# Short convolution, input projection: two 512-token products per weight slot, or seven products of halves

## The chip, the cores and the metric

The kernel runs on one core of one Trainium2 chip. The metric is the device time of one execution in microseconds (us), as the median of the runs shown. A difference of under about 0.2% (5.7 us here) can't be told from no change.

The engines are named as in the profile. PE is TensorE (PEld its weight loads), DVE is VectorE, ACT is ScalarE, POOL is GpSimd and SP is SyncE. SPq, DVEq and the like are the sequencers of these engines.

## What is computed

The program is a stack of six layers on 512 tokens of width 1024, all in float32. The first block has four attention layers. The second has a hybrid attention and state-space layer with a feed-forward layer, then a short convolution with a feed-forward layer. The change concerns the short convolution alone:

```python
def shortconv_mixer(h, w_in, conv_w, w_out):
    gb, gc, u = jnp.split(h @ w_in, 3, axis=-1)
    return (gb * dw_conv(gc * u, conv_w)) @ w_out
```

Here `h` is 512 x 1024 and `w_in` is 1024 x 3072, `dw_conv` is a depthwise convolution over tokens with three taps, and `w_out` is 1024 x 1024. The feed-forward layers, `(silu(h @ w_gate) * (h @ w_up)) @ w_down` with 2816 hidden columns, matter because they already use the scheme that the change brings to `h @ w_in`.

## The kernel before

Activations are held transposed, with 128 features on the partitions and tokens along the row. `h` has eight such tiles, and `T` is 512 tokens. PSUM has eight banks of 512 columns. Weights arrive through `ring`, two slots of 1 MB each. `load` on SP waits for the semaphore `slot_begun` and then issues the transfer into the slot that was freed. PE raises `slot_begun` at the first matmul that reads a slot.

**The short convolution, before.** Its weights are twelve slots of 256 output columns. They come in four groups `g`, each in the order gc, u, gb (`for part in (1, 2, 0)`, L623). On PE, `short_convolution` (L1680) runs `pair_of_tiles` (L739) for each slot: two tiles of 128 outputs in the two PSUM banks `TB`, and eight products over the 1024 inputs for each tile (L727). A float32 matmul leaves two records in the trace, so a slot is 32 records of 512 columns. ACT copies the gc tiles to `sc_gate` (L2247, recorded at L1769). DVE (L3150) multiplies each u tile by its gate into `sc_pad` (L3161), runs `convolve` (L2854, recorded at L2856 to L2858: a tensor_scalar and two scalar_tensor_tensor over 512 columns), and multiplies each gb tile by the result into `og` (L3169). The output projection (`out_projection_of_parts`, recorded at L921) reads `og`.

**The scheme of seven products.** In `ffn` (PE: L1627), a chunk is one slot: 1024 inputs by 256 outputs, for 512 tokens. Weights and activations are each cut into four quarters. DVE forms four sums of weight quarters for each slot (`sum_weights`, L3015, recorded at L3024, L3026, L3029 and L3031), and once for each layer four sums of activation quarters (`sum_moving`, L3037, recorded at L3044). PE then makes seven products of 512 inputs by 128 outputs by 256 tokens where a plain product would need eight (`first_parts` L1603, `other_parts` L1608, recorded at L1588). A part is 8 records of 256 columns, and a chunk is 56. Three results must be saved between parts. ACT copies them to `snaps` (L2225), and DVE adds them back (L3070, L3075 and L3077 in `gated_pair`). The last part of a chunk (`c.a22`, `t4`) waits until DVE has made the second of these additions (L1624). Two sets of three PSUM banks alternate.

In DVE's order of work, the four weight sums for the *next* chunk stand between the first and the second addition of the present one, and they wait until the next slot has arrived:

```python
nc.vector.tensor_tensor(put[0][:, early], r3, snaps[i][0], ALU.add).then_inc(S["sum_read"], ...)  # L3070
if i or not first:
    sum_weights(1 - i, 4)                                                                          # L3072
dve.wait_ge(S["part_done"], at.now(p7))
dve.wait_ge(S["snap_read"], snapped.now(4 * i + 3))
nc.vector.tensor_tensor(put[1][:, late], r1, snaps[i][2], ALU.add).then_inc(S["sum_read"], ...)    # L3075
```

The sums for the first chunk of a layer are made ahead, in `first_weights_of` (L3052).

**POOL.** It computes the conditioning vectors of later layers from `ada_w` in 24 steps for each layer, which it fetches itself (L657). A step is a tensor_scalar (L669) and a tensor_tensor (L673) over 1024 columns, all in SBUF. The steps for the first feed-forward layer's successor run from 1753.7 us and those for the last layer from 2186.5 us.

Of the kernel before, what the change touches and what calls it, by code (L numbers as in the profile page):

```python
# [20 lines left out]
T = 512  # L21
D = 1024
KT = D // P
# [7 lines left out]
ALU = mybir.AluOpType  # L31
ACT = mybir.ActivationFunctionType
# [200 lines left out]
def build(nc, A, out, tables, const):  # L233

    ctx = ExitStack()
    with ctx:
# [242 lines left out]
        sc_gate = view(0, 2, T)  # L479
        sc_pad = view(1024, 2, T + 2)  # L480
        sc_sum = view(2060, 2, T)

        block = ctx.enter_context(nc.Block())

# [209 lines left out]
        def _(pe):  # L694
# [932 lines left out]
            def ffn(job):  # L1627
# [118 lines left out]
        def _(act):  # L1746
# [567 lines left out]
        def _(dve):  # L2314
# [790 lines left out]
            def ffn(job):  # L3105
# [26 lines left out]
                for pair in range(KT // 2):  # L3132
                    for at in range(len(DOWN_CHUNKS)):
# [12 lines left out]

                        add_chunk(job, pair, at, between)
                add_square(KT - 2)

            def short_convolution():  # L3150
                for i in range(2):
                    for at in (0, T + 1):
                        settle(nc.vector.memset(sc_pad[:, i, at:at + 1], 0.0))
                group, row = col_at["sc_conv_w_2"]
                with turns(dve, 2, n, {"tile": 12, "dve_step": 8, "og_ready": 4}) as t:
                    for g in range(2):
                        skip(2)
                        for i in range(2):
                            tile = next_tile()
                            done(tile)  # L3160
                            nc.vector.tensor_tensor(sc_pad[:, i, 1:1 + T], tile.at, sc_gate[:, i, :], ALU.mult  # L3161
                                                    ).then_inc(tile_used[tile.bank], 1)
                            evacuated(tile)
                            taps = [cols[:, group, ds(t * 4 + (row + 8 * tap + 2 * g + i), 1)] for tap in range(3)]
                            convolve(sc_sum[:, i, :], sc_pad[:, i, :], T, taps)
                        for i in range(2):
                            tile = next_tile()
                            done(tile)
                            nc.vector.tensor_tensor(og[:, ds(t * (4 * T) + (2 * g + i) * T, T)], tile.at, sc_sum[:, i, :],  # L3169
                                                    ALU.mult).then_inc(tile_used[tile.bank], 1)  # L3170
                            evacuated(tile)
                            dve.sem_inc(S["og_ready"], n.give("og_ready"))

            def block2_vector():
                dve.wait_ge(S["rms_ready"], n.take("rms_ready"))
# [125 lines left out]
```

## Time and profile before

| | us |
|---|---|
| median of 3 runs | 2848.48 (2845.95 to 2850.03) |
| the profiled execution's own time | 2844.35 |
| its span, first to last instruction | 2842.5 |
| input projection of the short convolution | 2184.5 to 2349.2 |
| first feed-forward layer, up to its end | 1753.2 to 2177 |
| last feed-forward layer, begins at | 2412.3 |

| engine | busy us | share of the span |
|---|---|---|
| PE | 2699.3 | 95% |
| PEld | 1768.6 | 62% |
| DVE | 1314.0 | 46% |
| ACT | 659.5 | 23% |
| POOL | 1069.4 | 38% |

The mean granted clock of PE is 0.98 of full speed. "Busy" counts instructions that are under way, and the matmul records overlap, so that starts tell more than sums. A row of instructions gives the engine, the line in the kernel, output and inputs by name, shapes, the count, the busy time and the mean of one, and behind the bar how long the engine stood idle before them and what it had waited for. A row of the timeline gives start and duration in us, and in brackets the idle time before it with its releaser.

### The profile page before, as it was taken

The numbers are of one execution on the slowest core, as the hardware profiler recorded it, in microseconds if no ns is written. First come the engines' busy times: TensorE is split into PE (matmuls) and PEld (weight loads), VectorE is DVE, ScalarE is ACT, GpSimd is POOL, SyncE is SP. The second block draws the span as 40 slices with busy tenths as digits, with TensorE's granted clock in tenths as the row PEclk, the third lists the DMA queues.
The fourth block names the chain that finished last, engine by engine and source line by source line (L and its number), as shares of the span: only waits on it lengthen the run. The fifth ranks groups of instructions, "written<-read, shape, count | busy, mean of one in ns | idle before, by whom it ended". The sixth has DMA issues, their size and how long they took to land.

```text
span 2842.5 us, 32196 instructions
## 1 busy us (share of the span) xinstructions
PE 2699.3 (95%) x11791; PEld 1768.6 (62%) x11791; DVE 1314.0 (46%) x2667; ACT 659.5 (23%) x1575; POOL 1069.4 (38%) x574
## 2 busy tenths in 40 slices
PE   6799999998999999899998899899999999999997
PEld 5356544465666544465645565788887444888886
DVE  7133367334556643333555663443554322433554
ACT  2133123322333432232214522111101001111101
POOL 4785188048583005850683002870001880000000
PEclk7899999999999999999999999999999999999999
DMA  7342343145342114332441003452223542222222
GB/s 244 106 129 92 95 131 115 59 117 147 83 126 53 30 45 124 115 94 59 120 140 38 1 16 99 147 153 89 85 82 99 164 148 74 74 89 85 83 88 71
DMA packets 245112, 277.81 MB, mean 98 GB/s; under 512 B 41427, under 2 KB 217824, under 8 KB 244864
## 3 DMA queue, kind: packets, MB, share of 16 engines
q1 hardware_dynamic: 216000, 175.03, 20.3%
q0 software_dynamic: 28224, 100.86, 11.5%
q8 instruction: 78, 1.28, 0.2%
q14 instruction: 42, 0.34, 0.0%
q10 hardware_dynamic: 768, 0.30, 0.0%
HBM read 274.06 MB, written 2.10 MB: 97 GB/s over the span
## 4 chain that ended last, share of the span: by engine, by line
PE 86%; DVE 4%; DMA 3%; ACT 2%; issue 2%; POOL 1%; SPq 1%; DVEq 0%; ACTq 0%; POOLq 0%
PE psum L1588 27%; PE psum L727 20%; PE psum L921 12%; PE psum L1101 7%; PE psum L895 3%; PE psum L1267 2%; PE psum L782 2%; PE psum L1285 1%; PE psum L907 1%; PE psum L1060 1%; PE psum L1061 1%; PE psum L1419 1%; PE psum L1123 1%; DMA ring<-in_ffn_w_gate 1%; POOL ada_ring L669 1%
## 5 line engine op out<-in xcount | busy, mean ns | idle before, releaser
L657 POOL DMA_DIRECT2D ada_ring<-in_ada_w x192 | 114.8, 598 | 1251.9 <-DVEq L2401 803.6
L727 PE MATMUL psum<-h,ring 128*128 128x512 f32 (+1 forms) x1280 | 538.9, 580 | 16.2 <-DVE arena L2345 4.7
L669 POOL TENSOR_SCALAR ada_ring<-ada_ring,cond 128x1024 f32<-128x1024 f32 x168 | 479.7, 2856 | 8.4 <-POOL ada_sum L673 2.1
L727 PEld LDWEIGHTS psum<-h,ring 128*128 128x128 f32 x1280 | 243.1, 192 | 295.4 <-issue 277.0
L673 POOL TENSOR_TENSOR ada_sum<-ada_sum,ada_ring 128x1024 f32<-128x1024 f32 x168 | 396.9, 2363 | 14.9
L921 PE MATMUL psum<-og,ring 128*128 128x512 f32 x768 | 334.9, 595 | 0.3
L1588 PE MATMUL psum<-og,arena 128*128 128x256 f32 x1152 | 258.6, 379 | 1.7 <-ACT probs L2225 1.7
L921 PEld LDWEIGHTS psum<-og,ring 128*128 128x128 f32 x768 | 145.2, 191 | 180.1 <-issue 180.1
L1588 PEld LDWEIGHTS psum<-og,arena 128*128 128x128 f32 x1152 | 218.7, 190 | 32.1 <-issue 2.4
L1101 PE MATMUL psum<-h,ring 128*128 128x512 f32 x496 | 229.4, 593 | 1.4 <-DVE arena L2473 1.4
L1819 ACT ACTIVATE probsT<-psum 128x128 f32<-128x128 f32 (+3 forms) x232 | 104.5, 451 | 338.9 <-PE psum L895 338.4
L1588 PE MATMUL psum<-h,ring 128*128 128x256 f32 x768 | 178.5, 383 | 1.6 <-DVE mods L2399 0.9
L1588 PEld LDWEIGHTS psum<-h,ring 128*128 128x128 f32 x768 | 146.2, 192 | 26.2 <-ACT h L1784 5.1
L2499 DVE CUSTOM_DVE_ANT_0 psum<-psum,cst 128x128 f32<-128x128 f32 (+1 forms) x192 | 95.3, 498 | 121.3 <-PE psum L1267 83.2
L1101 PEld LDWEIGHTS psum<-h,ring 128*128 128x128 f32 x496 | 87.8, 191 | 81.8 <-issue 81.0
L1852 ACT ACTIVATE sq<-x 128x512 f32<-128x512 f32 x63 | 39.8, 631 | 424.7 <-DVE x L2565 228.4
L2225 ACT ACTIVATE probs<-psum 128x256 f32<-128x256 f32 x132 | 50.8, 385 | 373.5 <-PE psum L1588 373.5
L3101 DVE SCALAR_TENSOR_TENSOR x<-psum,mods,x 128x256 f32<-128x256 f32 x168 | 81.2, 483 | 112.1 <-PE psum L1588 110.8
L2565 DVE SCALAR_TENSOR_TENSOR x<-psum,mods,x 128x512 f32<-128x512 f32 x48 | 36.0, 751 | 204.3 <-PE psum L921 203.8
L1808 ACT ACTIVATE psum<-psum,neg_max 128x256 f32<-128x256 f32 (+3 forms) x256 | 122.7, 479 | 23.7 <-DVE neg_max L2499 22.1
L895 PE MATMUL psum<-cst,arena 128*128 128x128 f32 x608 | 110.9, 284 | 10.6 <-ACT probsT L1819 7.0
L1769 ACT ACTIVATE arena<-psum 128x512 f32<-128x512 f32 (+4 forms) x100 | 55.1, 558 | 281.9 <-PE psum L727 228.8
(387 smaller groups left out, 3818.0 us busy)
## 6 DMA issues: line engine op xcount, KB each, us to landing
ada_ring<-in_ada_w POOLq DMA_DIRECT2D x192, 512.0 KB, 4.1
ring<-in_ffn_w_gate SPq DMA_DIRECT2D x22, 1024.0 KB, 5.3
ring<-in_ffn_w_up SPq DMA_DIRECT2D x22, 1024.0 KB, 5.4
ring<-in_ffn_w_down SPq DMA_DIRECT2D x16, 1024.0 KB, 5.2
ring<-in_sc_w_in SPq DMA_DIRECT2D x12, 1024.0 KB, 5.8
ring<-in_mla_w_in SPq DMA_DIRECT2D x10, 1024.0 KB, 5.5
ring<-in_mla_w_out SPq DMA_DIRECT2D x8, 1024.0 KB, 5.1
ring<-in_swa_w_in SPq DMA_DIRECT2D x16, 512.0 KB, 5.5
```

The costliest lines, as they stand in the source:

```text
L657: pool.dma_start(ada_ring[:, i % 2, :], w[k * P:(k + 1) * P, first(part)]).then_inc(arrived[i % 2], n.give(f"ada_in{i % 2}", 16))
L669: step = nc.gpsimd.tensor_scalar(piece, ada_ring[:, i % 2, :], c, None, ALU.mult)
L673: step = nc.gpsimd.tensor_tensor(total, total, piece, ALU.add)
L727: m = pe.matmul(tile.at[:, part], lhs(k), rhs(k), start=(k == 0), stop=(k == K - 1))
L895: m = pe.transpose(bank[:, i * P:(i + 1) * P], p[:, block_at:block_at + P], ident)
L921: m = pe.matmul(out_tiles[c].at, w8(out_slots[0], P * (c % 2))(k), og[:, k * T:(k + 1) * T], start=(k == 0), stop=(k == KT - 1))
L1101: m = pe.matmul(made["tile"].at, weights(made)(k), h_lat(k), start=(k == 0), stop=(k == KT - 1))
L1588: last = pe.matmul(out, weights[:, k, :], moving[:, k, :], start=begins and k == 0, stop=True, skip_group_check=True)
L1808: e = nc.scalar.activation(scored, scored, ACT.Exp, bias=neg_max[:, step % 4, g:g + 1], scale=scale, accum_out=row_sum[:, step % 4, g:g + 1])
L1819: c = nc.scalar.activation(probsT[:, i % 2, 0:w], PB[:, 0:w], ACT.Copy)
L2499: last = nc.vector.tensor_tensor_reduce(s[:, at:at + w], s[:, at:at + w], mask(u), -scale, floor, ALU.add, ALU.min, neg_max[:, b, g:g + 1])
L3101: nc.vector.scalar_tensor_tensor(xq, bank, scales[q], xq, ALU.mult, ALU.add).then_inc(S[told], n.give(told))
```

## The change

The twelve slots of the short convolution become twelve chunks of seven products. Chunk `c` belongs to group `c // 3` and is of kind `c % 3`: 0 is gc, 1 is u and 2 is gb. The weights, their order and the loads stay.

- PE: `short_convolution` runs chunks as in `ffn`. The first two are started together, then one follows the other. It waits for the last DVE and ACT reads of all twelve before the output projection.
- The extra `slot_begun` at the end of the first feed-forward layer (`frees_slot`) lets the second slot of the short convolution load earlier.
- ACT: in place of eight copies of 512 columns, three copies of 256 for each chunk.
- DVE: four sums of `h` quarters into `sc_moving` and four weight sums for each slot. For each chunk it makes three additions and puts the gates on: a copy for kind 0, products with `sc_gate` for kind 1, products with `sc_sum` for kind 2. For kind 1, two convolutions follow the last product, before the next chunk's first addition.
- The weight sums of chunk 0 are made at the end of the feed-forward layer before.

```diff
@@ PE
-                result_squares(job)
+                result_squares(job, frees_slot=job is not None)
 
             def short_convolution():
-                for i in range(12):
-                    pair_of_tiles(fresh=(i == 0))
...
+                first, second = chunk(0), chunk(1)
+                for bank in (0, 1):
+                    evacuated_last(bank)
+                first_parts(first, slot_begins=False, fresh=h0)
+                first_parts(second, slot_begins=False)
+                other_parts(first, moving_ready=t0 + 3)
+                other_parts(second, slot_begins=True)
+                for c in range(2, SC_CHUNKS):
+                    pe.wait_ge(S["snap_read"], snap0 + 3 * (c - 1))
+                    pe.wait_ge(S["sum_read"], sum0 + 4 * (c - 1))
+                    following = chunk(c)
+                    first_parts(following)
+                    other_parts(following)
+                pe.wait_ge(S["snap_read"], snap0 + 3 * (SC_CHUNKS - 1))
+                pe.wait_ge(S["sum_read"], sum0 + 4 * (SC_CHUNKS - 1))
...
@@ ACT
-                with turns(act, 2, n, {"tile": 12}):
-                    for g in range(2):
-                        for i in range(2):
-                            copy_tile((sc_gate[:, i, :], whole))
-                        skip(4)
+                for c in range(SC_CHUNKS):
...
+                    for snap, (part, bank) in enumerate(((p1, r1), (p6, r1), (p5, r2))):
+                        act.wait_ge(S["part_done"], begun + part)
+                        nc.scalar.activation(snaps[c % 2][snap], bank, ACT.Copy).then_inc(S["snap_read"], n.give("snap_read"))
...
@@ DVE
+                if job == 6:
+                    first_weights_of("sc")
...
+                for which, k in ((1, 4), (3, 8), (2, 8), (4, 8)):
+                    dve.wait_ge(S["h_ready"], h_at - KT + k)
+                    sum_moving(halves, sc_moving, which)
+                sum_weights(1, 4)
...
+                for c in range(SC_CHUNKS):
...
+                    dve.wait_ge(S["part_done"], begun + p2)
+                    dve.wait_ge(S["snap_read"], snapped + 3 * c + 1)
+                    nc.vector.tensor_tensor(put[0][:, early], r3, snap[0], ALU.add).then_inc(S["sum_read"], n.give("sum_read"))
+                    if 0 < c < SC_CHUNKS - 1:
+                        sum_weights((c + 1) % 2, 4)
+                    dve.wait_ge(S["part_done"], begun + p7)
+                    dve.wait_ge(S["snap_read"], snapped + 3 * c + 3)
+                    nc.vector.tensor_tensor(put[1][:, late], r1, snap[2], ALU.add).then_inc(S["sum_read"], n.give("sum_read"))
+                    dve.wait_ge(S["part_done"], begun + p3)
+                    nc.vector.tensor_tensor(put[0][:, late], r2, snap[1], ALU.add).then_inc(S["sum_read"], n.give("sum_read"))
+                    dve.wait_ge(S["sum_read"], n.now("sum_read"))
+                    if kind == 1:
+                        settle(nc.vector.tensor_tensor(put[0], put[0], factor[:, 0, :], ALU.mult))
...
+                    dve.wait_ge(S["part_done"], begun + p4)
...
+                    nc.vector.tensor_tensor(put[1][:, early], r1, factor[:, 1, early], ALU.mult
+                                            ).then_inc(S["sum_read"], n.give("sum_read"))
+                    last = nc.vector.tensor_tensor(put[1][:, late], put[1][:, late], factor[:, 1, late], ALU.mult)
...
+                    for i in range(2):
...
+                        settle(convolve(sc_sum[:, i, :], sc_pad[:, i, :], T, taps))
```

## Rows read from the trace of the kernel before

**Rows 1.** Busy time by stage: PE, PEld, DVE, ACT, POOL, PEclk, DMA.
```profile
1775.00:1912.00 137.00, 121.41 (x540) 103.51 (x540) 64.69 (x84) 17.88 (x44) 118.81 (x61) 0.96 0.49 152
1912.00:2049.00 137.00, 137.00 (x636) 120.62 (x635) 59.93 (x105) 21.11 (x50) 0.73 (x1) 1.00 0.29 92
2184.50:2349.20 164.70, 164.70 (x385) 73.06 (x385) 41.07 (x50) 9.45 (x16) 132.34 (x69) 1.00 0.48 153
```

**Rows 2.** Groups by line and shape, 2184.5 to 2349.2 us.
```profile
L727 PE MATMUL psum<-h,ring 128*128 128x512 f32 x384 | 165.0, 592 | 0.0
L2858 DVE SCALAR_TENSOR_TENSOR arena<-arena,cols 128x512 f32<-128x512 f32 x8 | 10.5, 1316 | 1.2 <-DVE arena L2857 0.2
L2857 DVE SCALAR_TENSOR_TENSOR arena<-arena,cols 128x512 f32<-128x512 f32 x8 | 10.2, 1274 | 1.2 <-DVE arena L2856 0.2
L2856 DVE TENSOR_SCALAR arena<-arena,cols 128x512 f32<-128x512 f32 x8 | 5.9, 733 | 1.2 <-DVE arena L3161 0.5
```

**Rows 3.** Timeline of DVE, two steady feed-forward chunks with POOL idle.
```profile
1922.20 0.42 DVE L3083 TENSOR_TENSOR arena<-psum,arena 128x256 f32 x1 [0.83 <-PE psum L1588]
...
1928.05 0.69 DVE L3024 TENSOR_TENSOR arena<-ring 128x512 f32<-128x512 f32 x1 [1.97 <-DMA ring<-in_ffn_w_up]
...
1930.82 0.42 DVE L3075 TENSOR_TENSOR arena<-psum,probs 128x256 f32<-128x256 f32 x1
...
1946.38 0.42 DVE L3083 TENSOR_TENSOR arena<-psum,arena 128x256 f32 x1 [0.83 <-PE psum L1588]
```

**Rows 4.** Groups by line and shape on DVE, 1775 to 1912 us, POOL busy.
```profile
L3031 DVE TENSOR_TENSOR arena<-ring,arena 128x512 f32<-128x512 f32 x10 | 18.3, 1834 | 0.3
L3026 DVE TENSOR_TENSOR arena<-ring 128x512 f32<-128x512 f32 x10 | 9.0, 900 | 0.0
L3029 DVE TENSOR_TENSOR arena<-arena,ring 128x512 f32<-128x512 f32 x10 | 9.0, 898 | 0.0
L3024 DVE TENSOR_TENSOR arena<-ring 128x512 f32<-128x512 f32 x10 | 7.4, 742 | 31.8 <-DMA ring<-in_ffn_w_gate 19.0 <-DMA ring<-in_ffn_w_up 12.8
L3081 DVE TENSOR_TENSOR arena<-arena 128x256 f32 x4 | 5.0, 1262 | 0.1
```

**Rows 5.** What PE waited for, 1775 to 1912 us: total, times, longest.
```profile
PE psum L1588 <- DVE arena L3075: 15.6, 8, 7.7
```

**Rows 6.** Timeline of POOL and DVE, two places with both at work.
```profile
1797.52 2.85 POOL L669 TENSOR_SCALAR ada_ring<-ada_ring,cond 128x1024 f32<-128x1024 f32 x1
...
1799.11 0.68 DVE L3026 TENSOR_TENSOR arena<-ring 128x512 f32<-128x512 f32 x1
...
1904.70 2.34 POOL L673 TENSOR_TENSOR ada_sum<-ada_sum,ada_ring 128x1024 f32<-128x1024 f32 x1
1904.82 2.77 DVE L3031 TENSOR_TENSOR arena<-ring,arena 128x512 f32<-128x512 f32 x1
```

**Rows 7.** Timeline, a convolution that no POOL instruction holds up.
```profile
2336.72 0.63 DVE L2856 TENSOR_SCALAR arena<-arena,cols 128x512 f32<-128x512 f32 x1
...
2338.40 0.75 DVE L2858 SCALAR_TENSOR_TENSOR arena<-arena,cols 128x512 f32<-128x512 f32 x1
```

**Rows 8.** Timeline of PE, first two chunks of both feed-forward layers.
```profile
1753.15 1.10 PE L1588 MATMUL psum<-h,ring 128*128 128x256 f32 x4 [0.46 <-DVE mods L2399]
...
1786.32 3.78 PE L1588 MATMUL psum<-og,ring 128*128 128x256 f32 x8 [7.66 <-DVE arena L3075]
1789.90 2.31 PE L1588 MATMUL psum<-h,ring 128*128 128x256 f32 x5
...
2412.33 1.10 PE L1588 MATMUL psum<-h,ring 128*128 128x256 f32 x4 [0.46 <-DVE mods L2399]
...
2439.95 3.19 PE L1588 MATMUL psum<-og,ring 128*128 128x256 f32 x8 [2.10 <-DVE arena L3075]
2442.93 4.15 PE L1588 MATMUL psum<-h,ring 128*128 128x256 f32 x16
```

**Rows 9.** Timeline of PE, two other gaps.
```profile
1156.59 7.11 PE L727 MATMUL psum<-arena,ring 128*128 128x512 f32 x12 [3.47 <-DMA ring<-in_mla_w_q_b]
...
1829.91 1.99 PE L1588 MATMUL psum<-og,ring 128*128 128x256 f32 x8 [2.20 <-DVE arena L3075]
```

More of the change, by code:

```diff
@@ L481, in build @@
         sc_sum = view(2060, 2, T)
+        sc_moving = [view(4096 + 1024 * i, 4, HALF) for i in range(4)]
+        SC_CHUNKS = 12
         block = ctx.enter_context(nc.Block())
@@ L1677, in ffn, with chunk @@
                 pe.wait_ge(S["sum_read"], n.of["sum_read"].at - 4)
-                result_squares(job)
+                result_squares(job, frees_slot=job is not None)
             def short_convolution():
-                for i in range(12):
-                    pair_of_tiles(fresh=(i == 0))
+                snap0, sum0 = n.of["snap_read"].at, n.of["sum_read"].at
+                MARK["ffn", "sc"] = (slots[0], n.of["slot_full0"].at, n.of["slot_full1"].at)
+                h0 = n.take("h_ready", KT) - KT
+                moving = halves_of(h[:, :, 0:T], 4)
+                t0 = n.of["moving_summed"].at
+                n.take("moving_summed", 4)
+                def chunk(c):
+                    return Chunk(open_slot(), 4, c % 2, moving, sc_moving, lambda k: snap0 + 3 * c + k,
+                                 lambda k: sum0 + 4 * c + k)
+                first, second = chunk(0), chunk(1)
[13 more added lines that the diff above has]
+                pe.wait_ge(S["sum_read"], sum0 + 4 * (SC_CHUNKS - 1))
+                n.take("snap_read", 3 * SC_CHUNKS)
+                n.take("sum_read", 4 * SC_CHUNKS)
             def block2_tensor():
@@ L3154, in short_convolution @@
                 group, row = col_at["sc_conv_w_2"]
[L3155 to L3172, printed above, removed]
@@ new lines, in short_convolution @@
+                h_at = n.of["h_scaled"].at
+                halves = halves_of(h[:, :, 0:T], 4)
+                for which, k in ((1, 4), (3, 8), (2, 8), (4, 8)):
+                    dve.wait_ge(S["h_ready"], h_at - KT + k)
+                    sum_moving(halves, sc_moving, which)
+                sum_weights(1, 4)
+                begun, snapped = n.of["part_done"].at, n.of["snap_read"].at
+                for c in range(SC_CHUNKS):
+                    g, kind = c // 3, c % 3
+                    p1, p2, p6, p5, p7, p3, p4 = FIRST_PARTS_DONE[c] if c < 2 else [7 * c + k for k in PARTS_DONE[0]]
+                    r1, r2, r3 = [psum[:, b, early] for b in BANK_SETS[c % 2]]
+                    snap = snaps[c % 2]
+                    put = [[sc_gate[:, q, :] for q in range(2)], [sc_pad[:, q, 1:1 + T] for q in range(2)],
+                           [og[:, (2 * g + q) * T:(2 * g + q + 1) * T] for q in range(2)]][kind]
+                    factor = [None, sc_gate, sc_sum][kind]
+                    dve.wait_ge(S["part_done"], begun + p2)
[11 more added lines that the diff above has]
+                        settle(nc.vector.tensor_tensor(put[0], put[0], factor[:, 0, :], ALU.mult))
+                    elif kind == 2:
+                        nc.vector.tensor_tensor(put[0], put[0], factor[:, 0, :], ALU.mult
+                                                ).then_inc(S["og_ready"], n.give("og_ready"))
+                    dve.wait_ge(S["part_done"], begun + p4)
+                    if kind == 0:
+                        nc.vector.tensor_copy(put[1][:, early], r1).then_inc(S["sum_read"], n.give("sum_read"))
+                        dve.wait_ge(S["sum_read"], n.now("sum_read"))
+                        continue
+                    nc.vector.tensor_tensor(put[1][:, early], r1, factor[:, 1, early], ALU.mult
+                                            ).then_inc(S["sum_read"], n.give("sum_read"))
+                    last = nc.vector.tensor_tensor(put[1][:, late], put[1][:, late], factor[:, 1, late], ALU.mult)
+                    if kind == 2:
+                        dve.wait_ge(S["sum_read"], n.now("sum_read"))
+                        last.then_inc(S["og_ready"], n.give("og_ready"))
+                        continue
+                    settle(last)
+                    dve.wait_ge(S["sum_read"], n.now("sum_read"))
+                    for i in range(2):
+                        taps = [cols[:, group, row + 8 * tap + 2 * g + i:row + 8 * tap + 2 * g + i + 1] for tap in range(3)]
+                        settle(convolve(sc_sum[:, i, :], sc_pad[:, i, :], T, taps))
@@ L3174, in block2_vector @@
+                n.take("part_done", 7 * SC_CHUNKS)
+                n.take("snap_read", 3 * SC_CHUNKS)
             def block2_vector():
```

5 lines of the change are left out of this document (added).

## The prediction, made before the changed kernel was run

> **What bounds the kernel now.** I read the stages first, then the groups of the stretch that changes, then the place where the kernel already does what the change brings. In the short convolution's input projection PE is busy for all of 164.7 us at full clock and never waits [rows 1, 2]. Each slot takes 164.7 / 12 = 13.7 us. DVE works only 41 us of it [rows 1]. So PE alone sets this stretch, and fewer products do shorten it, as long as nothing else becomes late. What could become late is seen in the first feed-forward layer, which runs the same chunks. With POOL idle, PE is busy 137.0 of 137.0 us. In the 137 us before, with POOL busy for 118.8 us, PE is busy only 121.4 us [rows 1], and its 15.6 us of waiting all ended on DVE's second addition (L3075) [rows 5]. In the short convolution POOL is busy for 132.3 of 164.7 us [rows 1]. The place to copy prices from is therefore the disturbed stretch, not the quiet one.
>
> **What it removes.** Twelve slots at 13.7 us become twelve chunks. Two steady quiet chunks take 1946.38 - 1922.20 = 24.18 us [rows 3], so one takes 12.09 us and a part 1.73 us. Twelve are 145.1 us: PE's own work falls by 19.6 us. ACT's eight copies go and thirty-six shorter ones come. Such copies never held PE in the steady chunks [rows 1, 5], so I cost them at nothing; the cover is that ACT worked only 9.5 us here, and without it each would stand once or twice in a chunk's order.
>
> **What it adds on DVE, and where that lies.** The last of the seven parts waits for the second addition. It is due 6 parts = 10.36 us after the chunk's start. Ahead of that addition stand the first addition and the four weight sums for the next slot, which wait for their load. Quiet: the sums begin 5.85 us after the chunk's start and the second addition stands at 8.62 us, 1.3 us before it would hold PE [rows 3]. With POOL at work the four sums have means of 1.83, 0.90, 0.90 and 0.74 us, together 4.4 us (spacing 0.2 us less, 4.2), against about 2.7 us quiet [rows 3, 4]. The reason is seen in single rows: the sum that begins 0.12 us after a POOL tensor_tensor takes 2.77 us in place of 0.69. Inside a POOL tensor_scalar there is no such hold: a sum that begins 1.6 us into one of 2.85 us takes 0.68 us [rows 6].
>
> The Trainium skill ("SBUF — State Buffer", section "Who interferes with whom") says that a DVE instruction with two SBUF inputs and a GpSimd instruction that reads SBUF exclude each other, and that the later one is fully blocked until the first has finished. The trace agrees for POOL's tensor_tensor and not for its tensor_scalar. The rule in full is the last rival below.
>
> *Ordinary chunks.* After a chunk of kind 0 or 2, DVE is free again some 1 to 3 us into the next one, so these behave as the disturbed feed-forward chunks: 15.6 - 7.7 = 7.9 us over ten chunks, 0.8 us each [rows 5, 8]. There are six among chunks 2 to 10 (3, 4, 6, 7, 9, 10): 4.8 us. Bounds: 0 and 2.2 us each [rows 3, 9].
>
> *The chunk after a convolution.* Here the change puts something new in DVE's order. From the end of a kind-1 chunk until the second addition of the next one, DVE must do: start up 0.2; the early product, 0.34 from start to start; the late product, two SBUF inputs, as L3081 with 1.26 and a wait of 0.15 [rows 4]; two convolutions; the first addition 0.34; the sums 4.2; the second addition with the signal to PE 0.5. A convolution in this very stretch of the kernel before has means of 0.73, 1.27 and 1.32 us with waits of 0.15 before each, 3.75 us [rows 2], where an undisturbed one takes 2.4 [rows 7]; two are 7.5. The sum is 0.2 + 0.34 + 1.4 + 7.5 + 0.34 + 4.2 + 0.5 = 14.5 us, against 10.3 due. PE stalls 4.2 us. Before, these convolutions cost nothing, since PE waits for no DVE work there [rows 2]; their cover is gone, because the next slot's sums and the addition that PE needs are queued behind them. Four chunks follow a convolution: 2, 5, 8 and 11. Chunk 11 has no next slot to sum and comes out at 10.3, just in time. So 3 x 4.2 = 12.6 us. Bounds: undisturbed the chain is 0.2 + 0.34 + 0.6 + 5.0 + 0.34 + 2.7 + 0.5 = 9.7, no stall; with a hold on the long side in each group I take 6 us.
>
> *The clock.* After PE's gap of 7.66 us its next 8 records take 3.6 us in place of 1.73, and after the one of 2.10 us they take 3.0 [rows 8]. After 3.47 us twelve records take 7.11 us where 384 took 0.429 each, so 2.0 us are lost; after 2.20 us none [rows 9]. That is the lower level, 1.2 of 2.4 GHz, for a few us. Gaps of 4.2 us should mostly meet it: 1.5 us each, 4.5 us in all (0 to 6).
>
> *The first two chunks.* In the feed-forward layers the way from the first matmul to chunk 2 is 1789.90 - 1753.15 = 36.8 us with POOL at work and 2442.93 - 2412.33 = 30.6 us with POOL idle, against 24.2 for steady chunks; the third slot's load can be issued only when the second chunk's other parts begin, and its sums stand ahead of L3075 [rows 8]. The same code comes here with POOL at work, but without the silu on ACT between the two chunks, for which I take off 0.8 us. I take 32.5 us, a little under the middle of 33.7 (ends 29.8 and 36).
>
> *Edges.* The sums for chunk 0 at the end of the feed-forward layer, some 2.7 us, fall into the time in which DVE waits for PE and ACT to make the root of the mean square, and I cost them at nothing; were they late, the whole 2.7 us would count. At the end PE waits for DVE's last product before the output projection: 0.7 us (0.6 to 2). POOL's own steps are needed only at the end of the output projection, 55 us after it is done, so its delays cost nothing.
>
> **The sum.** 32.5 + 10 x 12.09 + 4.8 + 12.6 + 4.5 + 0.7 = 176.0 us, against 164.7: 11.3 us longer. The profiled execution's own time of 2844.35 becomes 2855.7. It lies 4.1 us under the median of the runs, so the forecast for the median is 2848.5 + 11.3 = 2859.8 us. The saving of 19.6 us is spent three times over: in the first pair, in the stalls behind the convolutions and in the other chunks.
>
> **The rivals.**
> - *The convolutions are hidden* (holds happen to miss them, POOL's steps and the chunks falling into a favourable rhythm). Then all chunks behave as the disturbed feed-forward ones: 32.5 + 120.9 + 9 x 0.8 + 0.7 = 161.3, 3.4 us shorter, 2845.1. For it: undisturbed the chain fits, with 0.6 us to spare. Against: it must fit three times, and POOL works in all of the stretch.
> - *PE sets the pace throughout* (the other side). The mechanism is that DVE's slack of 1.3 us per chunk holds, as in the quiet chunks [rows 3]. 29.8 + 120.9 + 0.7 = 151.4, 13.3 us shorter, 2835.2. It decides if the weight sums take under 3.9 us from the load's landing and the chain behind a convolution under 10.3. Against it stand the 15.6 us of waits [rows 5].
> - *Longer stalls:* the rhythm is unfavourable, each late chunk delays the next load and half-clock stretches add up: 36 + 120.9 + 6 x 1.5 + 3 x 6 + 6 + 2 = 191.9, 27 us longer, 2875.7.
> - *Each POOL instruction holds DVE for its whole length.* POOL's two instructions are 2.86 and 2.35 us of a step of some 6.7 us, so DVE's two-input work gets about 1.5 us per step. The chain behind a convolution has 7 us of such work, five steps, some 33 us, a stall of over 20 us three times: at least 60 us slower, over 2900. The skill's page above would have it so. Against: the sum that ran at 0.68 us inside a POOL tensor_scalar [rows 6].
>
> **How the numbers follow.** The forecast's mechanism has a chance of 0.62 (3 to 23 us slower), hidden convolutions 0.20, PE sets the pace 0.08, longer stalls 0.08, the full hold 0.02. Faster by over 0.2% (5.7 us, about what a measurement can tell) takes the pace case and a fifth of the hidden case: 0.12. Within 0.2% is the rest of the hidden case and the forecast's low end: 0.20. Slower is 0.68. The range of 8 in 10 runs from 2843, which leaves out the pace case, to 2872.
>
> **What would show it right or wrong.** Right: PE waits on the second addition in chunks 2, 5 and 8 for some 4 us each and hardly in chunk 11; under 1 us in the others; from the first matmul to chunk 2 some 32 us; a granted clock under 1.00 in the stretch; DVE's convolutions directly ahead of the late sums. Wrong: if the gaps are all under 1 us, the holds were overrated; if PE waits on loads or on ACT, I missed a resource; if the stretch is long without gaps, the price of a part is off.

## The result, and the profile after

The changed kernel takes 2857.77 us (median of 20 runs, 2853.46 to 2865.10), the kernel before 2848.84 in as many runs beside it (2841.84 to 2859.24). The ratio is 1.003, with an interval of 1.0021 to 1.0039: some 9 us slower, where 11.3 were forecast. The profiled execution took 2858.88 us, with a span of 2856.9. The line numbers have moved: L1588 is now L1590, the three additions are L3206, L3211 and L3213, the weight sums L3056, L3058, L3061 and L3063, the convolution L2888 to L2890, POOL's two operations L671 and L675, and the output projection L923.

First the stretch by stage, from the first product to L923 (columns as in [rows 1]), then what PE waited for in it (total, times, longest):

```profile
2185.10:2363.80 178.70, 155.64 (x672) 132.63 (x673) 116.10 (x142) 16.82 (x42) 135.61 (x69) 0.94 0.44 136
```

```profile
PE psum L1590 <- DVE og L3211: 13.2, 3, 5.6
PE psum L1590 <- DVE arena L3211: 9.8, 5, 4.3
PE psum L1590 <- ACT h L1812: 1.4, 1, 1.4
```

The stretch took 164.7 us before [rows 1] and takes 178.7 now, 14.0 us more. PE has less to do, and waits eight times for DVE's second addition, 23.0 us in all. The three waits on `og` are chunks 2, 5 and 8, the ones behind a convolution. PE's timeline gives the place of each (start, duration, records, and in brackets the idle time before it):

```profile
2185.13 7.58 PE L1590 MATMUL psum<-h,ring 128*128 128x256 f32 x32 [1.37 <-ACT h L1812]
...
2212.55 3.56 PE L1590 MATMUL psum<-arena,ring 128*128 128x256 f32 x8 [4.30 <-DVE arena L3211]
2215.95 3.62 PE L1590 MATMUL psum<-h,ring 128*128 128x256 f32 x16
...
2232.03 3.78 PE L1590 MATMUL psum<-arena,ring 128*128 128x256 f32 x8 [5.56 <-DVE og L3211]
...
2247.28 1.99 PE L1590 MATMUL psum<-arena,ring 128*128 128x256 f32 x8 [0.83 <-DVE arena L3211]
...
2278.61 3.78 PE L1590 MATMUL psum<-arena,ring 128*128 128x256 f32 x8 [4.74 <-DVE og L3211]
...
2324.05 2.90 PE L1590 MATMUL psum<-arena,ring 128*128 128x256 f32 x8 [2.90 <-DVE og L3211]
...
2362.11 1.89 PE L1590 MATMUL psum<-arena,ring 128*128 128x256 f32 x8
```

Behind a gap of 0.83 us eight records take 1.99 us, at a granted clock of 1.00; behind 4 to 6 us they take 3.6 to 3.8, at a granted clock of 0.50 to 0.53, which is the lower level. The wait in chunk 1 (4.30 us) is the one on the third slot's load, which landed 23.5 us after the start:

```profile
2208.63 0.69 DVE L3056 TENSOR_TENSOR arena<-ring 128x512 f32<-128x512 f32 x1 [6.29 <-DMA ring<-in_sc_w_in]
```

Chunk 2 begins at 2215.95, so the first pair takes 30.8 us. The last chunk's last part at 2362.11 follows without a gap. The waits come to 23.0 us, and the longer durations behind the four long gaps (against 1.99 for 8 records and 3.62 for the 16 that follow) to 8.1. With 12 x 12.09 = 145.1 that is 176.2 of the 178.7; the rest is 0.3 us at each gap. This is DVE's chain in chunk 2, and POOL beside it:

```profile
2212.87 2.74 DVE L3216 TENSOR_TENSOR arena<-arena 128x512 f32<-128x512 f32 x1
2216.22 0.42 DVE L3225 TENSOR_TENSOR arena<-psum,arena 128x256 f32<-128x256 f32 x1 [0.62 <-PE psum L1590]
2216.56 1.30 DVE L3227 TENSOR_TENSOR arena<-arena 128x256 f32<-128x256 f32 x1
2217.90 1.69 DVE L2888 TENSOR_SCALAR arena<-arena,cols 128x512 f32<-128x512 f32 x1
2219.63 2.71 DVE L2889 SCALAR_TENSOR_TENSOR arena<-arena,cols 128x512 f32<-128x512 f32 x1
2222.38 0.75 DVE L2890 SCALAR_TENSOR_TENSOR arena<-arena,cols 128x512 f32<-128x512 f32 x1
...
2226.11 0.42 DVE L3206 TENSOR_TENSOR og<-psum,probs 128x256 f32<-128x256 f32 x1
2226.45 2.46 DVE L3056 TENSOR_TENSOR arena<-ring 128x512 f32<-128x512 f32 x1
2228.84 0.68 DVE L3058 TENSOR_TENSOR arena<-ring 128x512 f32<-128x512 f32 x1
2229.44 0.68 DVE L3061 TENSOR_TENSOR arena<-arena,ring 128x512 f32<-128x512 f32 x1
2230.16 1.49 DVE L3063 TENSOR_TENSOR arena<-ring,arena 128x512 f32<-128x512 f32 x1
2231.57 0.41 DVE L3211 TENSOR_TENSOR og<-psum,probs 128x256 f32<-128x256 f32 x1
```

```profile
2219.40 2.40 POOL L675 TENSOR_TENSOR ada_sum<-ada_sum,ada_ring 128x1024 f32<-128x1024 f32 x1
...
2226.03 2.34 POOL L675 TENSOR_TENSOR ada_sum<-ada_sum,ada_ring 128x1024 f32<-128x1024 f32 x1
...
2229.78 3.06 POOL L671 TENSOR_SCALAR ada_ring<-ada_ring,cond 128x1024 f32<-128x1024 f32 x1
```

DVE is without a break at work from 2216.22 to 2231.98. L2889 and L3056 each begin 0.2 to 0.4 us after one of POOL's tensor_tensors and take 2.71 and 2.46 us where 0.75 and 0.68 are their free durations. L3063 begins 0.4 us after a tensor_scalar and takes 1.49.

### The profile page after: what moved, and what is told of

Read it like the earlier page. It is cut to its first block, busy times and chain, and to the rows that moved or that the text cites. A ratio compares the mean times of both kernels' runs of the same rounds, so it can differ in the third digit from the quotient of the medians.

```text
span 2856.9 us, 32856 instructions
## 1 busy us (share of the span) xinstructions
PE 2690.6 (94%) x12079; PEld 1829.3 (64%) x12079; DVE 1380.5 (48%) x2767; ACT 665.1 (23%) x1603; POOL 1072.6 (38%) x574
## 4 chain that ended last, share of the span: by engine, by line
PE 83%; DVE 6%; DMA 4%; issue 3%; ACT 2%; POOL 1%; SPq 1%; DVEq 0%; ACTq 0%; POOLq 0%
PE psum L1590 29%; PE psum L729 14%; PE psum L923 12%; PE psum L1103 7%; PE psum L897 3%; PE psum L1269 2%; PE psum L784 2%; PE psum L1287 1%; PE psum L909 1%; DMA ring<-in_sc_w_in 1%; PE psum L1062 1%; PE psum L1063 1%; PE psum L1421 1%; PE psum L1125 1%; PE psum L1146 1%
## 5 line engine op out<-in xcount | busy, mean ns | idle before, releaser
L671 POOL TENSOR_SCALAR ada_ring<-ada_ring,cond 128x1024 f32<-128x1024 f32 x168 | 480.7, 2861 | 8.4 <-POOL ada_sum L675 2.1
L675 POOL TENSOR_TENSOR ada_sum<-ada_sum,ada_ring 128x1024 f32<-128x1024 f32 x168 | 398.4, 2372 | 14.9
L729 PE MATMUL psum<-h,ring 128*128 128x512 f32 (+1 forms) x896 | 378.2, 580 | 17.5 <-ACT arena L1797 5.1
L923 PE MATMUL psum<-og,ring 128*128 128x512 f32 x768 | 333.3, 593 | 0.3
L729 PEld LDWEIGHTS psum<-h,ring 128*128 128x128 f32 x896 | 171.9, 195 | 207.8 <-issue 188.8
L1590 PE MATMUL psum<-og,arena 128*128 128x256 f32 x1152 | 258.6, 379 | 1.7 <-ACT probs L2253 1.7
L923 PEld LDWEIGHTS psum<-og,ring 128*128 128x128 f32 x768 | 144.7, 190 | 178.4 <-issue 178.4
L1590 PEld LDWEIGHTS psum<-og,arena 128*128 128x128 f32 x1152 | 219.1, 190 | 31.7 <-issue 2.4
L1590 PE MATMUL psum<-h,ring 128*128 128x256 f32 x960 | 224.7, 386 | 3.0 <-ACT h L1812 2.1
L1590 PEld LDWEIGHTS psum<-h,ring 128*128 128x128 f32 x960 | 185.0, 194 | 34.3 <-ACT h L1812 5.8
L1590 PE MATMUL psum<-arena 128*128 128x256 f32 x640 | 148.0, 379 | 0.0
L1103 PEld LDWEIGHTS psum<-h,ring 128*128 128x128 f32 x496 | 88.0, 191 | 81.7 <-issue 80.9
L1590 PE MATMUL psum<-h,arena 128*128 128x256 f32 x576 | 136.1, 379 | 0.0
L1590 PEld LDWEIGHTS psum<-arena 128*128 128x128 f32 x640 | 121.8, 190 | 16.3
```

Of the source, the lines that this page charges most:

```text
L671: step = nc.gpsimd.tensor_scalar(piece, ada_ring[:, i % 2, :], c, None, ALU.mult)
L675: step = nc.gpsimd.tensor_tensor(total, total, piece, ALU.add)
L729: m = pe.matmul(tile.at[:, part], lhs(k), rhs(k), start=(k == 0), stop=(k == K - 1))
L923: m = pe.matmul(out_tiles[c].at, w8(out_slots[0], P * (c % 2))(k), og[:, k * T:(k + 1) * T], start=(k == 0), stop=(k == KT - 1))
L1103: m = pe.matmul(made["tile"].at, weights(made)(k), h_lat(k), start=(k == 0), stop=(k == KT - 1))
L1590: last = pe.matmul(out, weights[:, k, :], moving[:, k, :], start=begins and k == 0, stop=True, skip_group_check=True)
```

## Experiments

The theory (Q): what PE waits for is DVE's work queued ahead of the second addition, stretched by POOL's holds. The first expectations call it H, for the holds. Rivals were the slots' loads (L), too much DVE work behind a convolution, held or not (D), too much DVE work in all with the holds (W), and, for the orders tried later, that a gain in one place is given back in another under POOL (R). Medians are of all runs of a kernel; ratios are against the kernel before in runs beside it.

**POOL's arithmetic left out, in both kernels.** For this POOL's loops around its steps are written out, here and where fewer bytes are fetched; the kernel before, at 1.0001 with both, shows no cost of that.

```
 pool.sem_inc(S["pool_awake"], 1)
+if last:   # the last layer's 24 steps: signals and fetches stay, no tensor_scalar, no tensor_tensor
+    ...
+    continue
```

> The changed kernel, where POOL fetches the last layer's ada_w as always but leaves out its 45 arithmetic instructions on them (so the last layer's conditioning is wrong). Its fetches then follow one another more densely than before. Theory H (DVE is held by POOL's SBUF instructions): no sum of weights above 0.75 us in the short convolution, no wait of PE on L3211 after the first two chunks, the stretch from the first matmul of the projection to the output projection falls from 178.7 to about 151 us, the time to about 2831 us. Rival L (the loads of the weight slots arrive late because POOL's fetches share the DMA engines): the loads stay late, PE goes on waiting and the stretch stays above 170 us, the time above 2850. Rival D (DVE has simply too much work behind a convolution, held or not): the waits in chunks 2, 5 and 8 stay at some 2 us or more, stretch some 160 us, time some 2840.

> The kernel before with the same arithmetic of POOL left out. PE waits for nothing there, so all theories expect the stretch to stay at 164.7 us and the time at 2848 to 2850 us. The difference to the changed kernel without this arithmetic is what the seven products are worth alone: 13 us by theory H (14.8 of PE work and edges), 5 or less by rivals L and D.

Changed kernel: 2832.08 us (5 runs), ratio 0.9938 [0.9910, 0.9965]. Kernel before: 2845.48 (10 runs), ratio 1.0001 [0.9981, 1.0022]. PE's waits in the changed one (L3216 is the second addition there):

```profile
PE psum L1595 <- DVE arena L3216: 3.6, 2, 3.1
PE psum L1595 <- ACT h L1817: 1.4, 1, 1.4
PE psum L1595 <- DVE og L3216: 0.9, 2, 0.5
```

The 23.0 us of waits became 4.5, and the stretch 152.8 us. The four sums took 2.6 us in every chunk. The loads landed after 6.4 us in the median, against 6.1 with POOL's arithmetic, so the waits did not go by earlier loads. Nor did DVE's work behind a convolution (D) hold PE by itself: chunks 2, 5 and 8 waited 0, 0.47 and 0.47 us. The same arithmetic costs nothing in the kernel before, whose PE needs no DVE work here, and some 26 us in the changed one. Without it the change is worth 13 us, near the 13.3 of the rival in which PE sets the pace. The longest wait left, 3.1 us in chunk 1, is on the third slot's load.

**Fewer bytes fetched by POOL.** Eight of each 1024 columns of the last layer's conditioning weights are fetched, so that its conditioning vector is not computed rightly; the arithmetic stays.

```
-pool.dma_start(ada_ring[:, i % 2, :], w[k * P:(k + 1) * P, first(part)]
+few = slice(0, 8) if last else slice(0, CHUNK)
+pool.dma_start(ada_ring[:, i % 2, few], w[k * P:(k + 1) * P, first(part)][:, few]
```

> The changed kernel, where POOL does all its arithmetic for the last layer but fetches only 8 of 1024 columns in each step (so that these sums are wrong): its instructions keep their pace while its traffic is nearly gone. Theory H: the slots land in about 5.4 us after issue in place of 5.5 to 7, ordinary chunks stall a little less, chunks 2, 5 and 8 still stall 3 to 5 us; the stretch falls by 2 to 6 us, the time to 2852 to 2856. Rival L: all stalls go, stretch 151 us, time some 2831.

Measured: 2867.74 us (5 runs), ratio 1.0062 [1.0041, 1.0083]: slower, where a small gain was expected. The loads did land earlier, after 5.1 us, and the waits grew:

```profile
PE psum L1591 <- DVE og L3212: 20.1, 3, 10.4
PE psum L1591 <- DVE arena L3212: 6.4, 5, 3.2
```

POOL's step fell from 6.7 to 6.3 us: between its addition and its next fetch it stood idle for 0.3 us in place of 0.65 to 0.84 (why is not shown). So its holds came denser and at other phases. Two weight sums have means of 1.56 and 1.52 us here, against 1.16 and 0.96. Ahead of chunk 2's first addition the two convolutions took 12.7 us, against 8.2. The three waits behind convolutions were 10.4, 3.6 and 6.1 us, so the loads don't explain those. In the ordinary chunks rival L is half right. The sums there could begin 5.9 to 6.2 us after the chunk's start, where with all the fetches it was 5.8 to 8.1, and these chunks waited 2.6 us in all, against 5.5.

**Convolutions left out.** The output takes the product gc * u without its taps.

```
-factor = [None, sc_gate, sc_sum][kind]
+factor = [None, sc_gate, sc_pad[:, :, 1:1 + T]][kind]
...
-for i in range(2):
-    taps = ...
-    settle(convolve(sc_sum[:, i, :], sc_pad[:, i, :], T, taps))
```

> The changed kernel without the eight convolutions over 512 columns (24 DVE instructions); the last product of a group takes sc_pad in their place. Theory H with the prediction's step: chunks 2, 5 and 8 become ordinary, with waits of 0 to 2 us (0.9 on average) in place of 5.6, 4.7 and 2.9, and the half clock behind them goes; the stretch falls by some 10 us of waits and 6 us of clock to about 162 us, the time to about 2842. Rival L: the convolutions don't matter, since the loads are late; stretch within 3 us of 178.7.

Measured: 2840.38 us (10 runs), ratio 0.9972 [0.9953, 0.9992].

```profile
PE psum L1590 <- DVE arena L3211: 13.2, 7, 7.0
PE psum L1590 <- DVE og L3211: 1.8, 3, 0.8
```

Chunks 2, 5 and 8 wait 1.8 us in all instead of 13.2. So the convolutions stand in that wait, as the prediction had it. Chunk 1 waited 6.96 us here against 4.30, with no change in its own order. Its load landed 25.7 us after the start in place of 23.5, and one of its sums took 2.83 us in place of 1.60:

```profile
2204.26 0.69 DVE L3056 TENSOR_TENSOR arena<-ring 128x512 f32<-128x512 f32 x1 [7.72 <-DMA ring<-in_sc_w_in]
```

**One of the two convolutions moved** behind the next chunk's third addition, where it is needed only by the product after it. Nothing is left out.

```
-for i in range(2):
+for i in range(1 if g < 3 else 2):      # at the end of kind 1
     convolution(i)
...
 elif kind == 2:
+    if g < 3:
+        convolution(1)                  # behind the third addition of kind 2
```

> The changed kernel with one DVE order altered: of the two convolutions of a group only the first stays behind the last product of the kind-1 chunk; the second moves into the next chunk, behind its third addition (the last group keeps both in place). The work is the same. Theory Q (what counts is how much stands ahead of the second addition in DVE's queue): the chain of 14.5 us loses 3.75, so chunks 2, 5 and 8 wait 0 to 2 us in place of 5.6, 4.7 and 2.9, and the half clock behind them goes; chunks 3, 6 and 9 stay under 2 us. Some 10 us of waits and 6 of clock, time about 2842. Rival W (DVE's total work with the holds is too much for a group of three chunks): the waits move to chunks 3, 6 and 9, the sum of waits stays above 18 us and the time above 2853.

Measured: 2842.50 us (12 runs), ratio 0.9987 [0.9974, 1.0000]. The waits fall from 23.0 to 12.4 us, the three behind a convolution to 2.82, 1.18 and 0.58, and the stretch to 161.8 us. The order change alone gives back about 15 us with the same work on every engine, which too much work in all (W) can't explain.

**Chunk 1's order.** Its weight sums for chunk 2 go behind its third addition.

```
-if 0 < c < SC_CHUNKS - 1:
+if 1 < c < SC_CHUNKS - 1:
     sum_weights((c + 1) % 2, 4)
...
+if c == 1:                              # behind the third addition
+    sum_weights(0, 4)
```

> The changed kernel with one order altered: in chunk 1 the four weight sums for chunk 2, which wait for a load, stand behind the third addition, so that the last part of chunk 1 no longer waits for that load. Theory Q: the wait of 4.3 us in chunk 1 and the 1.7 us of half clock behind it go, and chunk 2's sums are still ready when its third part wants them (some 3.5 us after its start); the rest stays, time about 2852. Rival: the wait returns as one of the same length before chunk 2's third part, since the load is what is late; time as the changed kernel, 2857 to 2858.

Measured: 2858.04 us (10 runs), ratio 1.0037 [1.0021, 1.0054]: nothing gained. The wait in chunk 1 was gone, and these stood later:

```profile
2219.22 3.78 PE L1590 MATMUL psum<-arena,ring 128*128 128x256 f32 x8 [5.71 <-DVE og L3211]
...
2293.64 3.78 PE L1590 MATMUL psum<-arena,ring 128*128 128x256 f32 x8 [3.35 <-DVE arena L3211]
2313.66 3.52 PE L1590 MATMUL psum<-arena,ring 128*128 128x256 f32 x8 [4.68 <-DVE og L3211]
...
2343.98 3.68 PE L1590 MATMUL psum<-arena,ring 128*128 128x256 f32 x8 [2.77 <-DVE arena L3211]
```

Waits of 3.35 and 2.77 us in chunks 7 and 10 were 1.68 and none before the edit. In both the sums could begin only 8.7 and 8.3 us after the chunk's start, against 5.8 and 6.1 before the edit, since they waited for the load. The stretch is 181.3 us.

**The same edit without POOL's arithmetic.** The new order in chunk 1 and POOL's arithmetic left out, together (the last layer's conditioning vector is not computed).

> The changed kernel with two things changed: chunk 1's weight sums for chunk 2 stand behind its third addition (as in first_order), and POOL's arithmetic on the last layer's conditioning vectors is left out, its fetches kept (as in no_math_after, 2832.1 us; that conditioning vector is then not computed). It asks why first_order gained nothing although its wait in chunk 1 went. Theory R (the gain was lost to POOL's rhythm: chunks that came earlier fell otherwise under its instructions): without POOL's arithmetic nothing takes it back. The wait of 3.1 us in chunk 1 goes, with the half clock behind it, and the stretch falls from 152.8 to some 148.5 us; the time is 3 to 5 us under no_math_after, 2827 to 2829, a ratio of 0.992 to 0.993. Theory S (the sums in their new place make chunk 2 late by themselves, since they now stand ahead of chunk 2's own early work): a wait of 3 us or more in chunk 2 here too, and 2832 us.

Measured: 2826.44 us (6 runs), ratio 0.9924 [0.9906, 0.9943], against 0.9938 without the edit. The intervals overlap, so the medians alone don't settle it. In the traces the stretch falls from 152.8 to 150.9 us. That is 1.9 us kept of a wait of 3.1 and its half clock. Chunks 3, 5, 6 and 8 now wait 1.02, 1.49, 0.57 and 1.10 us, 4.2 in all, where 4.5 were waited before. Nothing held the sums (2.6 us each time); in these four chunks they began 8.1 to 9.0 us after the chunk's start, as the load came. So the wait came back at later loads without POOL's arithmetic, and R's reason, the holds alone, is not enough. That the arithmetic took back more (the stretch grew by 2.6 us with it) rests on one profile of each.

**The gate columns' bank.** PE's first product waited 1.37 us, by the profile for ACT's `h`. DVE's timeline shows the reader of a bank that this product needs, behind four tiles of `h`:

```profile
2182.08 2.72 DVE L2448 SCALAR_TENSOR_TENSOR h<-x,gains,psum 128x512 f32<-128x512 f32 x4 [0.59 <-PE psum L773]
2184.72 0.15 DVE L2431 TENSOR_TENSOR mods<-psum,cols 128x8 f32<-128x8 f32 x1
```

```
-if columns is not None and k == (1 if job in (6, 8) else 3):
+if columns is not None and k == (1 if job in (6, 7, 8) else 3):
```

> The changed kernel with the gate columns of the short convolution's layer read after the second tile of h, as in the layers with seven products, and not after the fourth. The profile names ACT's h as what PE waited for (1.37 us) before its first product. Theory G: it is really the bank that these gate columns occupy, which the new code waits for and the old one did not; then the first product starts 1 to 1.4 us earlier after the norm, and ACT's tiles later set the pace, so 0.5 to 1.4 us are gained. Rival A: it is ACT, as the profile says, and the start stays where it is. Neither can be seen in the time of one run, only in the trace.

One run: 2860.8 us, which says nothing of so small a time. From the sum of squares (L766) to the first product it took 7.89 us against 8.80 (7.39 in the kernel before), and the wait's label became that reader:

```profile
2186.10 1.10 PE L1590 MATMUL psum<-h,ring 128*128 128x256 f32 x4 [0.46 <-DVE mods L2431]
2187.55 7.45 PE L1590 MATMUL psum<-h,ring 128*128 128x256 f32 x28 [0.35 <-ACT h L1812]
```

The 0.9 us are real, and the name that the profile gave was only that of the signal that came last.

**The three orders together.**

> All three orders together: one convolution moved, the first pair's sums moved, the gate columns early. Theory Q: the gains add, some 16 + 6 + 1 us, time about 2835, under both kernels: the seven products then bring some 11 to 14 us against the kernel before. Rival W: above 2848.

Measured: 2841.67 us (12 runs), ratio 0.9984 [0.9968, 1.0000]: the same as the moved convolution alone, where Q had 2835. The stretch is 162.7 us with 10.5 us of waits on additions. The gains did not add up here.

**And the feed-forward layers' first pair,** in the same order, added to the three, and alone in the kernel before.

```
-if i or not first:
+if not first:
     sum_weights(1 - i, 4)
...
+if first and i:                         # behind the third addition
+    sum_weights(0, 4)
```

> three_orders (2841.7 us) with one more change of order: in both feed-forward layers, as in chunk 1 of the short convolution, the second chunk's weight sums for the third stand behind its third addition. Nothing is left out. In three_orders these layers' second chunks wait 4.6 us (first layer, POOL at work) and 2.0 us (last layer, POOL idle), and some half clock follows each. Theory R: where POOL is idle the gain of about 3.3 us is kept; in the first layer most is given back, 0 to 2 us stay. 2836.5 to 2838.5 us. Theory S (the order loses by itself what it gains, POOL or not): 2841.7. If nothing is given back anywhere: 2832.

> The kernel before with the same change of order in both feed-forward layers' first pair, nothing else; nothing is left out. Its waits there are 7.66 us (first layer, POOL at work) and 2.10 us (last layer, POOL idle), with about 2 and 1.3 us of half clock behind them. Theory R: 3.3 us are kept in the last layer, and 0 to 3 of the 9.6 us in the first: 2842.5 to 2845.5 us. If nothing is given back: 2836. Theory S: 2848.8.

Measured: 2828.26 us (6 runs), ratio 0.9924 [0.9906, 0.9942], and 2834.96 us (6 runs), ratio 0.9953 [0.9936, 0.9970]. Both are beyond what theory R allowed. The first layer's second chunk in the kernel before with the edit, whose wait was 7.66 us [rows 8], now has no gap:

```profile
1774.11 1.89 PE L1588 MATMUL psum<-h,arena 128*128 128x256 f32 x8
1775.83 1.89 PE L1588 MATMUL psum<-og,ring 128*128 128x256 f32 x8
1777.56 3.62 PE L1588 MATMUL psum<-h,ring 128*128 128x256 f32 x16
```

From its first product to the next sum of squares (L764) this layer takes 414.5 us against 424.0 before, and the last layer 403.2 against 407.3. That is 9.6 + 4.1 = 13.6 us, and 13.5 were measured. The first layer's own length scatters: 421.6 to 436.7 us in the eleven profiles without this edit, 414.5, 416.0 and 417.0 in the three with it. So a gain is clear there, with POOL at work, and its size is not exact. R fits the short convolution and is wrong as a rule.

**The sums behind the second addition** from chunk 2 on, without the moved convolution, the other orders kept.

```
-if 0 < c < SC_CHUNKS - 1:
-    sum_weights((c + 1) % 2, 4)
...
 nc.vector.tensor_tensor(put[1][:, late], r1, snap[2], ALU.add)...   # second addition
+if 1 < c < SC_CHUNKS - 1:
+    sum_weights((c + 1) % 2, 4)
```

> four_orders without split_conv's edit, and in its place another order in the short convolution: from chunk 2 on the weight sums for the next chunk stand directly behind the second addition instead of ahead of it (chunk 1's stay behind the third). Nothing is left out. Theory Q (PE's waits are DVE's work queued ahead of the second addition): behind a convolution that chain falls from 14.5 by the sums' 4.2 to 10.3 us, just in time; the sums then begin about 10.9 us after a chunk's start and end near 15.1, and the next chunk's third part needs them at 12.1 + 3.5 = 15.6. So waits of some 0 to 1 us a chunk, a stretch of 150 to 157 us against 164.0 in four_orders, and 2816 to 2822 us. Rival M (the wait only moves: the sums, held by POOL, are late for the third part): waits on the last sum of 1 to 2 us a chunk in place of those on the second addition, and 2826 to 2832 us.

Measured: 2830.86 us (8 runs), ratio 0.9948 [0.9929, 0.9968]: a miss, not better than four_orders. PE's waits:

```profile
PE psum L1590 <- DVE og L3211: 8.2, 3, 4.0
PE psum L1590 <- DVE mods L2431: 0.5, 1, 0.5
PE psum L1590 <- DVE arena L3063: 0.4, 1, 0.4
```

The ordinary chunks wait for nothing, as Q had it, and the wait on the last sum is 0.4 us, not rival M's. But chunks 2, 5 and 11 waited 4.01, 2.08 and 2.10 us. My expectation had left something out. The sums now stand in the kind-1 chunk, ahead of its product and its convolutions, and delay the chain's start instead of standing in it. In chunk 2 it looked like this (L3220 is the product, L2888 to L2890 the convolutions):

```profile
2201.28 2.88 POOL L675 TENSOR_TENSOR ada_sum<-ada_sum,ada_ring 128x1024 f32<-128x1024 f32 x1
2201.86 2.85 DVE L3220 TENSOR_TENSOR arena<-arena 128x512 f32<-128x512 f32 x1
2204.74 0.42 DVE L3229 TENSOR_TENSOR arena<-psum,arena 128x256 f32<-128x256 f32 x1
...
2205.56 1.41 DVE L2888 TENSOR_SCALAR arena<-arena,cols 128x512 f32<-128x512 f32 x1
...
2208.58 2.55 DVE L2888 TENSOR_SCALAR arena<-arena,cols 128x512 f32<-128x512 f32 x1
```

The stretch was 159.3 us in this one profile, against 164.0 in that of four_orders, while the medians stand the other way round with overlapping intervals. Which of the two orders is better is open.

## Why the prediction was right

The sign, the size and the place came out as forecast. Point by point:

- **PE's own work.** Without gaps a chunk takes 12.09 us here as well (chunks 10 and 11). Without POOL's arithmetic the change is worth 13 us, so the saving was real and was spent elsewhere.
- **Behind a convolution:** 12.6 us forecast, 13.2 measured (5.56, 4.74, 2.90). Counted from the chunk's start, the chain was 10.36 us and these, 14.8 in the mean, against 14.5. Its terms were less near. Ahead of these three chunks the two convolutions took 8.2, 10.3 and 7.6 us, 8.7 in the mean, where 7.5 were taken from a mean of all four groups [rows 2]. The four sums took 5.2, 3.2 and 3.3 us, 3.9 in the mean against 4.2, and the products ahead of the convolutions 1.3 against 1.7. So part of the agreement is errors that cancel. That this chain is the cause is shown by conv_out and split_conv.
- **Ordinary chunks:** 4.8 forecast, 5.5 measured, but otherwise spread: four of the six waited 0.83 to 1.89 us, and chunks 9 and 10 not at all. Chunk 10 had no POOL beside its sums: they ran from 2345.80, and POOL's last instruction ended at 2345.16. The forecast took its price whole from the feed-forward chunks, and gave POOL's holds as the reason. The rows show a second part, the load: in chunks 3, 4, 6 and 7 it let the sums begin 8.1, 7.3, 7.5 and 5.8 us after the chunk's start, and they then took 3.2 to 6.0 us in place of 2.7. With POOL idle it is 6.1 us, and not the 5.85 of the prediction, which counts from DVE's first read [rows 3]; PE began that chunk 0.3 us earlier, as the first row below shows (kernel before). So the slack there is 1.0 us and not 1.3. That the sum of the ordinary chunks came so near is luck.

```profile
1921.90 3.62 PE L1588 MATMUL psum<-h,ring 128*128 128x256 f32 x16
```

```profile
2342.81 2.35 POOL L675 TENSOR_TENSOR ada_sum<-ada_sum,ada_ring 128x1024 f32<-128x1024 f32 x1
...
2345.80 0.69 DVE L3056 TENSOR_TENSOR arena<-ring 128x512 f32<-128x512 f32 x1 [1.99 <-DMA ring<-in_sc_w_in]
```

- **The first pair:** 30.8 us against 32.5. The wait in chunk 1 was 4.3 us, not the 7.66 that the first feed-forward layer showed [rows 8].
- **The clock:** three gaps behind a convolution cost 6.5 us at the lower level where 4.5 were taken. Here eight or more records ran slow behind each; the term was mis-sized by 0.7 us a gap.
- **The edges.** The tail cost nothing (0.7 forecast). From the sum of squares to the first product it took 8.80 us, against 7.39 before, so the start cost 1.4 us where nothing was forecast. The bank of the gate columns, which I had missed, is 0.9 of them, as gates_early showed; the other 0.5 us was not traced.
- **Chunk 11** was in time, as forecast, but for another reason: POOL had finished at 2345.16, nothing held its convolutions, and DVE stood idle for 3.1 us ahead of the second addition. The forecast's "just in time" under POOL was not put to the test.
- **The rival of a full hold,** at least 60 us slower, did not come: POOL's tensor_scalar holds DVE for a part of its length only. L3063, begun 0.4 us behind one, took 1.49 us, and was done 1.2 us before it. By the Trainium skill ("SBUF — State Buffer", "Who interferes with whom") the later of the two would be blocked until the first has finished. The trace again agrees for POOL's tensor_tensor (2.71 and 2.46 us in place of 0.75 and 0.68), and not for its tensor_scalar.

In sum 30.8 + 120.9 + 5.5 + 13.2 + 6.5 = 176.9, with 0.3 us at each of seven gaps 179.0, against the 176.0 of the forecast and 178.7 measured. The stretch grew by 14.0 us, 2.7 more than forecast, and the median by 8.9, 2.4 less. The two profiled executions differ by 14.5 us (2858.88 and 2844.35), which is the stretch and 0.5 ahead of it; the first lay 1.1 us over the median of its kernel and the other 4.5 under. Single executions scatter by more than this difference: the first feed-forward layer begins between 1742.9 and 1755.8 us in the profiles of these kernels, though nothing ahead of it was changed in any of them. Where that scatter comes from is open. The sign and the mechanism don't rest on it; how near the median came to the number does.

## What to carry to other kernels

A cheaper scheme on the bound engine must be paid for by the engine that helps it: list what is queued there ahead of the operation that the bound engine waits for, at the durations of a stretch with the same neighbours, not of a quiet one. Then look at the order before the amount of work. Edits of a few lines turned +9 us into -20 (2828.26 against 2848.43 us) with no instruction less. One convolution behind what PE needs brought 15 us. In the two feed-forward layers' second chunks the sums behind the additions brought 13 (2841.67 to 2828.26); the same in the short convolution brought nothing that can be measured. The edit in the feed-forward layers was to be had in the kernel before too, and was worth 13.5 us there. And price the load together with the work that waits for it: where an engine has 1.0 us to spare, a load that lands 2 us later and a hold of 2 us each use it up.

## What the runs showed of the hardware that was not expected

- A POOL instruction stream that cost nothing (ratio 1.0001 with it left out) cost 26 us as soon as PE waited for DVE beside it.
- Fetching less made the kernel slower (1.0062 against 1.003): POOL's step of 6.7 us became one of 6.3, and single waits went up to 10.4 us. Two kernels with the same DVE work behind a convolution waited 2.9 to 10.4 us. In chunk 2 the difference is in the holds: the two convolutions took 8.2 us in one and 12.7 in the other.
- POOL's fetches delay the loads of the slots: with 512 KB fetched in each step the sums could begin 5.8 to 8.1 us after an ordinary chunk's start, with 4 KB 5.9 to 6.2 (one profile of each).
- The lower clock level came behind gaps as short as 2.10 us (8 records in 3.19 us [rows 8], in 2.84 in sums_behind), but behind one of 2.82 us in split_conv the same records took 1.99. Rows alone don't tell which short gap will cost it.
